# Two heads interleaved on VectorE in differential attention: reciprocal before exponential bias, output norm between ratio and combination

## The reference, cut to what matters

```
s = einsum('bhcqd,bhckd->bhcqk', q, k) * (A_DQK ** -0.5)
p = softmax(s, axis=-1)
w = p[:, :, 0] - lam * p[:, :, 1]
o = einsum('bhqk,bhkd->bhqd', w, v)
o = rms_norm(o over the head's 64 values, g, eps=1e-5) * (1 - lam_init)
```

## Time and profile before

| what | value |
|---|---|
| median of three runs | 3162.82 us |
| the profiled execution | 3156.76 us, span 3154.9 us |
| TensorE matmul busy | 2883.1 us (91%) |
| VectorE busy | 1951.7 us (62%) |
| ScalarE busy | 1238.2 us (39%) |
| GpSimd busy | 561.6 us (18%) |
| mean granted TensorE clock | 0.961 |

### The profile page before, as it was taken

One profiled execution on the slowest core, in us unless ns is written; L12 is line 12 of the kernel. 1 busy time (PEld: TensorE's weight loads), 2 busy tenths in 40 slices (PEclk: granted clock), 3 DMA queues, 4 the chain that ended last, 5 costly groups with the idle time before them and its releaser, 6 DMA issues.

```text
span 3154.9 us, 47187 instructions
## 1 busy us (share of the span) xinstructions
PE 2883.1 (91%) x17730; PEld 1617.4 (51%) x17730; DVE 1951.7 (62%) x2706; ACT 1238.2 (39%) x2368; POOL 561.6 (18%) x449
## 2 busy tenths in 40 slices
PE   5999887888899999999998899987889999999997
PEld 3555643554545556757755554544554434444443
DVE  5976786882575304626646686778864673374765
ACT  5212456773543213313324311447753542231332
POOL 0021010001318101202212004010003160121211
PEclk8999996999999999999999799999989999999998
DMA  5211111221143321111141311113322432111133
GB/s 211 74 41 36 36 46 70 86 78 67 55 147 133 107 87 41 41 41 50 45 147 41 143 44 41 44 42 112 109 79 80 137 103 76 51 56 52 54 140 115
DMA packets 69316, 248.95 MB, mean 79 GB/s; under 512 B 9248, under 2 KB 10016, under 8 KB 69152
## 3 DMA queue, kind: packets, MB, share of 16 engines
q1 hardware_dynamic: 68000, 241.44, 22.6%
q10 hardware_dynamic: 1152, 5.24, 0.4%
HBM read 221.75 MB, written 19.92 MB: 77 GB/s over the span
## 4 chain that ended last, share of the span: by engine, by line
PE 60%; issue 20%; DVE 11%; ACT 5%; DMA 2%; POOL 1%; SPq 0%; DVEq 0%; POOLq 0%; ACTq 0%
PE PS L801 38%; PE PS L970 16%; DVE wlo L1925 3%; PE PS L822 2%; DVE R L2102 1%; ACT whi L1418 1%; DVE R L2089 1%; PE PS L1175 1%; ACT SW L1776 1%; DMA R<-in_w_ada 1%; DMA stage<-in_w_gu 1%; ACT X L1535 1%; ACT R L1533 1%; DVE X L2378 1%; PE PS L1220 1%
## 5 line engine op out<-in xcount | busy, mean ns | idle before, releaser
L801 PE MATMUL PS<-R,whi 128*128 128x512 f16 (+1 forms) x4992 | 1359.2, 360 | 47.1 <-DVE wlo L1925 30.8
L801 PE MATMUL PS<-R,wlo 128*128 128x512 f16 (+1 forms) x2496 | 896.4, 359 | 0.0
L801 PEld LDWEIGHTS PS<-R,whi 128*128 128x128 f16 x4992 | 487.5, 99 | 550.8 <-issue 51.7
L970 PE MATMUL PS<-R,whi 128*128 128x256 f16 (+2 forms) x2352 | 510.2, 326 | 0.3 <-DVE wlo L1938 0.3
L1925 DVE SCALAR_TENSOR_TENSOR wlo<-stage,whi 128x1024 f16<-128x1024 f32 (+1 forms) x204 | 283.4, 1390 | 362.0 <-ACT whi L1418 361.1
L801 PEld LDWEIGHTS PS<-R,wlo 128*128 128x128 f16 x2496 | 246.2, 99 | 242.5 <-issue 10.7
L970 PE MATMUL PS<-R,wlo 128*128 128x256 f16 (+2 forms) x1176 | 319.1, 326 | 0.0
L970 PEld LDWEIGHTS PS<-R,whi 128*128 128x128 f16 x2352 | 230.1, 98 | 152.5 <-DVE wlo L1938 0.8
L1418 ACT ACTIVATE whi<-stage 128x1024 f16<-128x1024 f32 (+1 forms) x204 | 210.4, 1032 | 135.3 <-PE PS L801 85.0
L2128 DVE TENSOR_REDUCE tiny<-PS 128x1 f32<-128x1280 f32 (+1 forms) x144 | 197.1, 1369 | 37.4 <-PE PS L998 35.7
L1954 DVE TENSOR_TENSOR X<-X,PS 128x256 f32<-128x256 f32 (+2 forms) x294 | 150.8, 549 | 93.4 <-PE PS L970 93.2
(11 more groups left out here) (227 smaller groups left out, 3570.3 us busy)
## 6 DMA issues: line engine op xcount, KB each, us to landing
stage<-in_w_gu SPq DMA_DIRECT2D x120, 512.0 KB, 3.8
X<-in_w_ada SPq DMA_DIRECT2D x60, 512.0 KB, 3.3
stage<-in_w_down SPq DMA_DIRECT2D x48, 512.0 KB, 3.4
stage<-in_w_in SPq DMA_DIRECT2D x44, 512.0 KB, 3.3
stage<-in_w_out SPq DMA_DIRECT2D x32, 512.0 KB, 3.2
h_save<-R SPq DMA_DIRECT2D x24, 640.0 KB, 5.3
R<-h_save SPq DMA_DIRECT2D x24, 640.0 KB, 4.9
T<-in_w_ada SPq DMA_DIRECT2D x20, 512.0 KB, 3.6
```

What stands on the lines that cost most here:

```text
L801: last = mm(slot(into, t0, t1)[:, c0 - t0:c1 - t0], w[:, j, k, :], row, start=(k == 0 and q == 0), stop=(k == K - 1 and q == 2))
L970: last = mm(s_bank(nf, t, o, n), w[:, j, k0 + k, :], row, start=(k == 0 and x == 0), stop=(k == PAIRS - 1 and x == 2))
```

## The change

`Chain` gets two new methods. `mark` raises the semaphore and returns its value, and does not wait; `reach` waits for such a value. With them the work on two heads is interleaved:

- the bias is taken out of `maxima(n, 0)` and becomes `bias`; the reciprocal is taken out of `combine` and becomes `inverse`;
- the order in head n is now maximum (n), reciprocal (n-1), bias (n), ratio (n-1), combination (n-1), maximum (n, 1);
- in h = 3 `out_norm` stands between ratio and combination instead of between bias and reciprocal;
- in h = 0 the scaling of the reciprocals stands between ratio and combination of the tile's last head instead of behind the combination.

No instruction that computes is added or removed, and each waits for the same results of the other engines.

```diff
+    def mark(self, ins):
+        ins.then_inc(self.s, 1)
+        self.k += 1
+        return self.k
+
+    def reach(self, k):
+        self.eng.wait_ge(self.s, self.base + k)
...
-                    own.link(red)
+                    return own.mark(red)
+
+                def bias(r, h, maximum):
+                    n = 4 * r + h
+                    own.reach(maximum)
                     if not (isinstance(r, int) and n < 2):
                         dve.wait_ge(s("exps"), 2 * n - 3 + before("exps"))
                     TS(nbias[:, h % 2, 0:1], smax[:, h % 2, 0:1], -SCORE, lamv[:, 12 + l:13 + l],
                        ALU.mult, ALU.add).then_inc(s("nbias"), 1)
 
-                def combine(r, h):
+                def inverse(r, h):
+
+                    dve.wait_ge(s("exps"), 2 * (4 * r + h) + 2 + before("exps"))
+                    return own.mark(nc.vector.reciprocal(rec[:, h, :], den[:, h % 2, :]))
+
+                def combine(r, h, inverted, norm=None):
 
                     n = 4 * r + h
-                    dve.wait_ge(s("exps"), 2 * n + 2 + before("exps"))
-                    own.link(nc.vector.reciprocal(rec[:, h, :], den[:, h % 2, :]))
-                    own.link(STT(beta[:, 0:1], den[:, h % 2, 0:1], lamv[:, 10 + l:11 + l], rec[:, h, 1:2], ALU.mult, ALU.mult))
+                    own.reach(inverted)
+                    ratio = own.mark(STT(beta[:, 0:1], den[:, h % 2, 0:1], lamv[:, 10 + l:11 + l], rec[:, h, 1:2], ALU.mult, ALU.mult))
+                    if h == HA - 1:
+                        own.mark(TS(rinv, rec[:, :, 0], 1.0 / XS, None, ALU.mult))
+                    if norm is not None:
+                        out_norm(norm)
+                    own.reach(ratio)
...
-                    if h == HA - 1:
-                        own.link(TS(rinv, rec[:, :, 0], 1.0 / XS, None, ALU.mult))
...
-                        maxima(r, h, 0)
-                        if h == 3 and not first:
-                            out_norm(r - 1)
+                        maximum = maxima(r, h, 0)
                         if h or not first:
-                            combine(*back(r, h, 1))
+                            inverted = inverse(*back(r, h, 1))
+                        bias(r, h, maximum)
+                        if h or not first:
+                            combine(*back(r, h, 1), inverted, r - 1 if h == 3 and not first else None)
                         maxima(r, h, 1)
```

More of the change, by code:

```diff
@@ L2194, in attend @@
                 own.leave(nt - 1, per)
-                combine(nt - 1, HA - 1)
+                combine(nt - 1, HA - 1, inverse(nt - 1, HA - 1))
                 out_sum(nt - 1)
```

## The result

The changed kernel took 3138.21 us in the median (3136.65 to 3139.98, four executions), the kernel before beside it 3159.59 us (3155.49 to 3166.67). The ratio is 0.9927 with a 95% interval of 0.9912 to 0.9942: 21 us or 0.7% faster. The forecast was 3154.9 us, 8 us faster, with a range from 3146: the direction was right and the size was not. In a second set of runs on another occasion the changed kernel had 3143.6 us against 3162.4, ratio 0.9938 (0.9922 to 0.9954), 19 us. The profiled execution of the changed kernel has a span of 3138.2 us.

The account below looks back on a forecast made before the run. Bound: a ring of waits per latent tile, held by VectorE in head 3. Terms -6.3 (latent tiles) - 0.3 (first tiles) + 0.1 (context) - 1.4 (clock) = -7.9 us, giving a median of 3154.9 us, range 3146 to 3164.

Parts of the forecast that it names:

- The ring: Latent tile's 24.76 us chain of waits: VectorE holds 9.06 us around head 3, so only savings there count, 0.41 + 0.04 us.
- Head 0's saving: Latent tiles, head 0: 0.21 us plus 0.29 from the moved scaling, counted as nothing because TensorE is late; bounds 0 to 0.5.
- head 2's scores held its maximum: Latent tiles, head 2: the second maximum waits for TensorE's scores, so of 0.21 us only 0 to 0.08 counts, taken as 0.04.
- The spacings: VectorE start-to-start times used as prices; in head 3 maximum to combination goes from 2.63 to 2.22 us, saving 0.41 us.
- The reciprocal ahead of the bias: Risk that the bias queues behind the reciprocal's wait for ScalarE in head 0: cost 0, bound 0.3 us a tile.
- the context tiles: Bias now between reciprocal and ratio: +0.09 us in five heads, norm gives back up to 0.34 once; +0.1 us taken.
- The tensor clock: Five of twelve tile distances ran at a lower clock, some 1.4 us each; one counted as gone, -1.4 us.
- the clock dips go: Rival, chance 0.14: with less idle time behind head 3 most of the five slow stretches vanish, -6.5 - 5.6, giving 3150.7 us.
- Waits for itself cost nothing: Rival, chance 0.15: VectorE's waits for its own results are free, so the new order has no effect, 3162.8 us.

Follow-up runs that it names:

- heads 0 to 2: The kernel before with the changed order of work only in heads 0, 1 and 2, head 3 as before; 3157.2 us, ratio 0.9982 to the kernel before.
- TensorE filled: The kernel before plus eight unread fp32 matmuls on TensorE in head 3 of each latent tile, VectorE untouched; 3147.7 us, ratio 0.9947 to the kernel before.
- head 3 alone: The kernel before with the changed order of work only in head 3; 3148.5 us, again 3145.5 us, ratios 0.9947 and 0.9949 to the kernel before.

## Why the prediction was wrong

**The ring: right.** Bound, place and size held: a tile is one stretch of VectorE in head 3 and two turns that don't hold it. Forecast 0.45 us a tile, measured 0.47 in layer 0 and 0.46 in layer 1. Head 0's saving ended in a wait for TensorE, head 2's scores held its maximum, and heads 0 to 2 alone moved the tile by 0.04 us.

**The spacings: nearly right.** Forecast 2.22 us from maximum to combination; measured 2.21 in layer 0 and 2.31 in layer 1, since the ratio came 0.22 us behind the bias there and not 0.14. In layer 1 the first maximum of head 3 moved up by itself, though: it starts 0.12 us behind the last step of `out_sum` now (2241.95 to 2242.07) and started 0.25 behind it before (2202.83 to 2203.08), where layer 0 had 0.11 already. I had not seen that gap, and what made it is not known.

**The reciprocal ahead of the bias: right.** In the loops of latent tiles of the changed kernel the list of waits has no entry of the reciprocal for ScalarE nor of an exponential for the bias. In the context tiles both wait, as forecast (VectorE's reciprocal and bias, then ScalarE's exponential in the changed kernel):

```profile
493.13 0.17 DVE L2153 RECIPROCAL st<-tiny 128x2 f32<-128x2 f32 x1 [0.47 <-ACT R L1573]
493.21 0.21 DVE L2147 TENSOR_SCALAR tiny<-tiny 128x1 f32<-128x1 f32 x1
```

```profile
493.46 0.47 ACT L1573 ACTIVATE R<-PS,tiny 128x256 f32<-128x256 f32 x1 [0.20 <-DVE tiny L2147]
```

It cost nothing there: outside the loop the bias stands only 0.08 us behind the reciprocal and fits into the wait that the ratio has anyway, and a context head takes 2.83 us as before. I had forecast 0.09 us a head.

**The tensor clock: wrong, and this is the step that failed.** "I count one of five gone, -1.4 us", within bounds of -7 and +12.6. Two profiles of before have 5 and 6 slow tiles, two of the change 1 and 1, so four or five tiles went back to the full clock and not one. Over the twelve distances of both loops the two profiles of before take 303.2 and 305.7 us, those of the change 291.6 both times: 12.9 us less in the mean, of which 12 x 0.47 = 5.6 is the ring and 7.3 the clock. The tails take 35.0 and 35.4 us against 29.5 and 32.4: 4.2 us more, for which I had no term at all. With the ring's two tiles outside the twelve distances (0.9) that is 18.0 us; the medians say 19 and 21. The remaining 1 to 3 us are in stretches whose length scatters by more than that from profile to profile.

The experiment with TensorE filled shows where the slow clock comes from rather than argues it: with VectorE's order and the tile's length unchanged, taking the idle time away in that one place removes every slow tile and shortens both tails, 16 us. That the change works through the same place is what "head 3 alone" and "heads 0 to 2" add. Two reasons for the misjudgement can be named. I knew where the slow stretches lay and that the change shortened the idle time ahead of them, and then took a small effect for a small cut. The idle time before the transposes went from 1.30 to 0.78 us in the layer 1 tiles shown here and from 1.59 to 1.03 in layer 0, and the slow tiles went from five or six of twelve to one. The idle time alone does not say which tile is slow. TensorE in layer 0, ahead of a full and of a slow tile of the kernel before, then in the changed kernel:

```profile
585.87 0.65 PE L1016 MATMUL PS<-ident,R 128*128 128x128 f32 x4 [1.59 <-DVE R L2147]
610.51 0.65 PE L1016 MATMUL PS<-ident,R 128*128 128x128 f32 x4 [1.59 <-DVE R L2147]
```

```profile
606.65 0.65 PE L1024 MATMUL PS<-ident,R 128*128 128x128 f32 x4 [1.03 <-DVE R L2168]
```

The wait is 1.59 us ahead of the full tile from 587.06 and ahead of the slow one from 611.69 (26.23 us at a clock of 0.93) alike. So the wait bears on how often the clock falls, and does not settle in which tile; what sets the moment stays open. The second reason: I priced the clock where I had looked, in the loop, and not in the tail, where the same matmuls ran at 0.68 to 0.84. Of the rivals, "the clock dips go" was the case that happened. It had a chance of 0.14 and a price of 12.1 us in all; with the 4.2 us of the tails that is 16.3 of the 19 and 21 measured.

**Waits for itself cost nothing: falls.** An instruction that doesn't need the maximum starts 1.41 us behind its start, one that does 1.61 to 1.62, in the same execution of the changed kernel. What the Trainium skill says in "VectorE: DVE Perf Modes", "The DRAIN you can't avoid", that a semaphore between two operations costs nothing extra, does not hold for this kernel's chain, where it costs 0.20 us behind the maximum. The same section also says that a next operation that is not held starts earlier, which the prediction left out and which agrees with the 1.41 us.

## What to carry to other kernels

Where TensorE waits in a ring, a small cut of the wait can return more than its own length, because fewer tiles behind it run at the low clock: here 0.47 us a tile came with four or five slow tiles of twelve less. Read the granted clock tile by tile, in loops and in their tails, and do not take its cost as proportional to the idle time. If slow tiles follow one certain wait, filling that wait with matmuls that nobody reads tests this in one run, and may be worth keeping. To interleave two heads' short operations pays where VectorE is on the ring, and only there: the same saving in three other heads gave 0.2% (0.0 to 0.4%).

## What was not expected of the hardware

A filler that does nothing useful made the old kernel 0.5% faster (0.9947, 0.9930 to 0.9963) and the changed one faster by another 0.3% (3134.0 against 3143.6 us beside it; 0.1% against its first runs). An fp32 product of 128 x 128 x 128 counts as two matmuls of 0.11 us each in the trace (8 products, 16 records, 1.95 us), where an fp32 transpose of the same size counts as one; three of the expectations had it at half its price. And the time of stretches that the change does not touch moves by 3 to 5 us between two profiles of one kernel (1453.8 and 1457.1 us between the attentions in the change, 1452.4 and 1457.9 before), so that one profile each of two kernels can't settle a difference of that size.
